# Leaving out the discarded matrix products in TensorE's waits at four layer-norm joints

## What is computed

```python
def layer_norm(x, g, b):
    mu = jnp.mean(xf, axis=-1, keepdims=True)
    var = jnp.mean(jnp.square(xf - mu), axis=-1, keepdims=True)
    return ((xf - mu) * lax.rsqrt(var + LN_EPS)).astype(x.dtype) * g + b

def post_norm_update(x, y, gate, res_w, g, b):
    return layer_norm(DN_ALPHA * x + res_w * gate * y, g, b)
...
    for i in range(DEPTH):                      # DEPTH = 2
        x = half_step_ffn(x, m[:, 0], m[:, 1], m[:, 2], ffn_w_in[i, 0], ...)
...
        hx = modulate(x, m[:, 3], m[:, 4])      # then neighbourhood attention (i = 0) or a short convolution (i = 1)
        x = post_norm_update(x, y_lat, m[:, 5], 1.0, ln_g[i, 1], ln_b[i, 1])
...
        x = half_step_ffn(x, m[:, 6], m[:, 7], m[:, 8], ffn_w_in[i, 1], ...)
    return x
```

## Time and profile before

| | |
|---|---|
| median of 3 runs | 2214.93 us (2208.83 to 2223.72) |
| profiled execution | 2212.52 us, of which the span from the first to the last instruction is 2210.7 us |
| TensorE busy | 2142.8 us (97%) |
| GpSimd busy | 1686.9 us (76%) |
| ScalarE busy | 1069.2 us (48%) |
| VectorE busy | 967.0 us (44%) |
| mean granted TensorE clock | 0.994 of full speed |

### The profile page before, as it was taken

The page is one execution under the profiler, slowest core; times in us unless marked ns, Lnnn a source line. Parts: engine busy times, 40 slices in busy tenths (PEclk is TensorE's granted clock), DMA queues, the critical chain, the costliest instruction groups (busy, mean ns, idle before and its releaser), DMA issues.

```text
span 2210.7 us, 32169 instructions
## 1 busy us (share of the span) xinstructions
PE 2142.8 (97%) x10197; PEld 1736.7 (79%) x10197; DVE 967.0 (44%) x1892; ACT 1069.2 (48%) x1646; POOL 1686.9 (76%) x1361
## 2 busy tenths in 40 slices
PE   9999999999999999999999999999999999999997
PEld 7787788777877887788778877787887788787886
DVE  7456676754556544553544442454112210434112
ACT  5555444355644543544544354555444444445442
POOL 6546498876464987888798888627988888797986
PEclk9999999999999999999999999999999999999999
DMA  7635487854344777777787865424665566464663
GB/s 257 166 106 191 153 282 244 290 176 143 108 170 153 273 260 297 255 267 264 278 284 257 314 203 165 146 75 143 195 200 186 165 186 212 140 218 146 197 205 118
DMA packets 135862, 447.10 MB, mean 202 GB/s; under 512 B 22538, under 2 KB 28130, under 8 KB 135768
## 3 DMA queue, kind: packets, MB, share of 16 engines
q1 hardware_dynamic: 130232, 427.24, 58.3%
q10 hardware_dynamic: 5536, 18.61, 2.4%
HBM read 444.60 MB, written 3.03 MB: 202 GB/s over the span
## 4 chain that ended last, share of the span: by engine, by line
POOL 50%; issue 26%; PE 21%; DVE 2%; POOLq 1%; ACT 0%; DMA 0%; SPq 0%; ACTq 0%; DVEq 0%
POOL w_lo L811 49%; PE ps L2155 6%; PE ps L2157 6%; PE ps L2156 6%; PE ps L2665 1%; PE ps L2653 1%; PE ps L2630 1%; PE ps L2493 1%; POOLq L194 0%; PE ps L2626 0%; POOL ada_land L857 0%; POOLq L809 0%; PE ps L2596 0%; PE ps L2406 0%; DMA cols<-cols_dram 0%
## 5 line engine op out<-in xcount | busy, mean ns | idle before, releaser
L811 POOL TENSOR_TENSOR w_lo<-land,w_hi 128x512 fp32r<-128x512 f32 x1300 | 1650.4, 1305 | 474.4 <-ACT w_hi L916 473.3
L916 ACT ACTIVATE w_hi<-land 128x1024 fp32r<-128x1024 f32 x654 | 692.4, 1061 | 914.8 <-PE ps L2157 692.8
L2155 PE MATMUL ps<-w_hi,h_hi 128*128 128x512 f32 (+1 forms) x1840 | 730.9, 397 | 37.4 <-DVE h_lo L1500 22.0
L2157 PE MATMUL ps<-w_hi,h_lo 128*128 128x512 f32 (+1 forms) x1840 | 718.6, 391 | 0.0
L2156 PE MATMUL ps<-w_lo,h_hi 128*128 128x512 f32 (+1 forms) x1840 | 717.7, 390 | 0.0
L2155 PEld LDWEIGHTS ps<-w_hi,h_hi 128*128 128x128 f32 x1840 | 346.6, 188 | 128.1 <-issue 40.2
L2157 PEld LDWEIGHTS ps<-w_hi,h_lo 128*128 128x128 f32 x1840 | 346.6, 188 | 73.6
L2156 PEld LDWEIGHTS ps<-w_lo,h_hi 128*128 128x128 f32 x1840 | 347.2, 189 | 67.3
L1542 DVE TENSOR_TENSOR hid_lo<-ps,hid_hi 128x512 f32 (+1 forms) x77 | 53.2, 691 | 548.3 <-ACT hid_hi L1056 548.3
L2155 PE MATMUL ps<-w_hi,hid_hi 128*128 128x512 f32 x616 | 245.4, 398 | 1.5 <-POOL w_lo L811 1.5
L2156 PE MATMUL ps<-w_lo,hid_hi 128*128 128x512 f32 x616 | 243.5, 395 | 0.0
(11 more groups left out here) (276 smaller groups left out, 1910.8 us busy)
## 6 DMA issues: line engine op xcount, KB each, us to landing
land<-ffn_w_in_dram SPq DMA_DIRECT2D x220, 512.0 KB, 3.6
ada_land<-ada_w_dram SPq DMA_DIRECT2D x144, 512.0 KB, 5.2
land<-ffn_w_out_dram SPq DMA_DIRECT2D x110, 512.0 KB, 3.9
land<-w_ffn_in_dram SPq DMA_DIRECT2D x88, 512.0 KB, 4.0
land<-w_ffn_out_dram SPq DMA_DIRECT2D x44, 512.0 KB, 4.6
land<-na_w_qkv_dram SPq DMA_DIRECT2D x40, 512.0 KB, 4.0
land<-w_xkv_dram SPq DMA_DIRECT2D x32, 512.0 KB, 3.5
land<-w_in_dram SPq DMA_DIRECT2D x32, 488.0 KB, 4.2
```

The costliest lines, as they stand in the source:

```text
L811: done = pool.tensor_tensor(w_lo[:, slot, half], land[:, slot, half], w_hi[:, slot, half].bitcast(F32), ALU.subtract)
L916: act.activation(w_hi[:, slot, :], land[:, slot, :], ACT.Copy).then_inc(*my.up("hi_ready"))
L2155: pe.matmul(dst, lh, wh, start=first, stop=False)
L2157: done = pe.matmul(dst, ll, wh, start=False, stop=last)
```

## The change

All three counts become zero, so `hold` issues nothing. No other instruction, wait or transfer is touched.

```diff
-HELD = (2, 2, 1)
+HELD = (0, 0, 0)
```

## The result

| | before | changed |
|---|---|---|
| median | 2214.93 us (2208.83 to 2223.72) | 2227.47 us (2224.36 to 2233.47) |
| profiled execution | 2212.52 us, span 2210.7 us | 2227.47 us, span 2225.7 us |
| TensorE busy | 2142.8 us | 2142.2 us |
| mean granted TensorE clock | 0.994 | 0.983 |

Five runs of each kernel give a changed kernel that is 0.52% slower, ratio 1.0052 with a 95% interval of 1.003 to 1.0074; the two medians are 12.5 us apart. The 19.1 us of held products are gone from TensorE, and its busy time is nearly what it was, because other products got longer.

A forecast was written before the change was run, and what follows sets the result against it. TensorE, busy 97% of the span, was taken to bound the kernel. Falls of 6.4 and 1.9 us, less 0.5 us given back, on 2212.52 us gave 2220.3 us, put at 2221 us; range 2210 to 2233 us.

The forecast's parts named there:

- the held products cost nothing and leave no gain: At the four joints: 19.1 us of held work lies inside waits set by ACT and DVE; removal gains 0.
- one stretch costs 1.6 us over dense products: Behind idle waits: a 3.4 us stretch at half clock slows 8 products by 0.20 us each, 1.6 us.
- I count one fall at each of the four joints: First and second wait around the transposes: one low-clock stretch per joint, 1.6 us each, 6.4 us in all.
- my second rival: Low clock for two stretches at each joint, all third waits falling too: 20.8 us, 2233 us; chance 0.10.
- slowed transposes: Transposes of tile 0 at low clock would delay DVE by 0.4 us, counted only in the 3.6 us upper bound.
- the third waits, 1.2 falls and 1.9 us: Waits of 1.84 us before tile 1: 0.3 falls a joint, 1.2 falls at 1.6 us each, 1.9 us.
- what is given back: Waits for POOL's `w_lo` about 15 us behind the joints absorb some delay: 0.5 us, bounds 0 and 1.5 us.
- the case that I gave 0.70: One low stretch at most joints, some behind the third waits: 2216 to 2226 us; chance 0.70.
- The added low time: Sign in the changed profile: added low-clock time over TensorE's work, divided by two, should equal the added span.
- one sign of being wrong: The prediction would be wrong if the clock fell at places far from the joints.
- Slower by over 1%: Rival: over 22 us lost, needing one low stretch beyond 44 us or all four beyond 11; chance 0.02.
- a low clock of 50 us: Skill's warning of a gate stuck slow: 25 us lost from one fall, 2238 us; not expected in this trace.

The follow-up runs named there:

- the still background: Kernel with all other waits held but the four joints empty, against the kernel before: ratio 1.0019, median 2220.32 us; 10.9 us above the same kernel with joints held.
- the version with (2, 2, 1): Also the held version: kernel before plus held products in RMS joint and attention waits, three moved to the 3.3 us wait: ratio 0.9962, median 2209.43 us.
- the version with (1, 1, 1): One held product at each place of the four joints, all other waits held, against the kernel before: ratio 0.9961, median 2210.25 us.

## Why the prediction was right or wrong

**Right: the held products cost nothing and leave no gain.** No wait became shorter without them, and the one joint without a fall in the kernel with the third wait empty lost 0.0 us.

**Right: the loss is the clock's, and one stretch costs 1.6 us over dense products.** Three joints with the third wait empty showed 1.6 us at the 16th to 20th product, and three with the second wait empty lost 1.57, 1.64 and 1.61 us.

**Wrong in size: "I count one fall at each of the four joints", 6.4 us.** A fall did come at each joint, but it was priced as one stretch, and the pair cost 9.9 us alone. Two stretches in a row came at all four joints, in the profile of the change as in that of the kernel with only the pair empty, and at three of four against the still background; the change had a third in a row at its fourth joint. The mechanism of my second rival, which I had given 0.10, is what happened; only its price of 3.6 us a joint was too high as a rule (the change lost 3.3 us at its fourth joint, with three stretches), since part of the first stretch lay in the wait, at the fourth joint of that kernel 3.1 of 3.4 us: the pair cost 2.05 to 2.90 us a joint when alone. I had read the five stretches of the trace as the form that a fall has. But those waits had dense work behind them, and here a second idle wait followed the first. With either of the two filled, the doubles were gone in seven of eight cases. Yet the second empty wait can't be the whole cause. The kernel with only the second wait empty had a double at its third joint, and the kernel with one product at each place had two elsewhere, behind single waits of 1.80 and 3.37 us with dense work behind them. What all 14 stretches of 6.8 us or more outside the neighbourhood attention have in common is that 0.6 to 2.5 us of waiting lies inside them, as 1.0 us does at the first joint of the change; the low stretches that lie wholly over products are all single there. Why the clock then stays low for longer is open.

**Named, but not put into the sum: slowed transposes.** I had 0.4 us for them in the upper bound alone. Where the clock was low under the transposes of tile 0, at the second and the fourth joint of the change, its first product came 0.20 and 0.43 us later after them than before; at the other two joints there was no such delay.

**Nearly right, by two errors that cancel: the third waits, 1.2 falls and 1.9 us.** There were two falls behind third waits with all left out, three with only the third empty and two against the still background, so 7 of 12, and not the 0.3 a joint that I took from the RMS joints. But the net loss was only 1.5 us for three.

**Wrong: what is given back.** I took 0.5 us for all four joints, from brackets of 0.47 us. A late TensorE got back 1.3 us behind the second and the third joint and 0.7 us behind the first. The two waits whose brackets say 0.25 and 0.47 us are 1.24 us from start to start. And it is given back only behind a fall at the third wait: in the change at the second and the fourth joint, where only the pair's stretches delayed TensorE, both waits for GpSimd are still there, here the second of them at the second joint, which answers to the earlier trace rows:

```profile
1739.72 0.50 PE L2155 MATMUL ps<-w_hi,h_hi 128*128 128x512 f32 x1 [0.46 <-POOL w_lo L811]
```

Slots of the ring are freed by the products of tile 1, so a delay in tile 0 delays ACT and GpSimd as well. That it is this which makes the difference was argued from the code and not tried.

**The sum.** Predicted 7.8 us over the profiled execution of before, measured 11.8 us from the first joint on, 12.5 us between the medians, and 10.9 us against the still background. The median of 2227.47 us is inside the range of 2210 to 2233 us and 6.5 us above the forecast. But it is inside only because the range reached up to the double stretches; it lies above the 2216 to 2226 us of the case that I gave 0.70, and two of the five runs, at 2233.47 us, reach just past the range.

**The signs that I had named.** The low clock behind every second wait, the 0.43 us and two falls behind third waits came as forecast. The added low time was to be twice the added span: at the joints it is 31.0 us over TensorE's work, half of it 15.5 us. Of that 2.0 us was given back behind the first and the third joint, and low time over the transposes costs only in part, which leaves the 11.8 us in reach. The waits for GpSimd are gone behind the third joint, and still there behind the second and the fourth. And one sign of being wrong came true by its words: the clock fell at places far from the joints, at 889 us and for longer in the attention. Kernels with the joints held show the same there, so it doesn't belong to the change; I should have asked for more low time than such kernels have.

**Slower by over 1%, and a low clock of 50 us.** The median is well below that; the two slowest runs are 0.8% above the median of before. The longest low stretch while TensorE worked was 20.5 us, in the attention of the kernel with the RMS joints held, about half of the 44 us at which I had set that rival, and six times what the rows of one trace had shown me. The 50 us that the Trainium skill warns of ("TensorE: Matmul & The Clock Gate", section "Part 1: The HAM clock gate") came up in no profile here. The Trainium skill's words there are that the gate was "stuck at K=1/4", which I took for the half-speed state; read as a quarter of full speed, my estimate from that page would have been 37.5 us and not 25. Every low stretch in these profiles is at 0.50.

## What to carry to other kernels

Where an engine with a gated clock waits between dense stretches, what counts is what stands behind the wait and whether a second wait follows: one stretch of 3.4 us at half clock costs 1.6 us over dense products and 0.5 to 0.6 us where most of it lies over discarded work, and two waits of over 2 us with eight transposes between them brought two in a row at 11 of 12 joints. One discarded product of 0.85 us in each wait of the joints was enough here (8 of 8 joints in two profiles), at no cost that could be seen, as long as it ends before the wait does; look in the timeline that it really stands where the queue waits. And price a stall from start to start, not by its bracket, before deciding how much of a delay it will take back.

## What the runs showed of the hardware that was not expected

**Short vector instructions beside GpSimd.** Spans of otherwise like kernels differ by 5 us from the first 40 us on, and the cause is in the start. Six of the 14 profiles have the longer one. These are DVE's rows of the version with (2, 2, 1), whose profiled execution took 2205.25 us:

```profile
19.84 0.18 DVE L1439 TENSOR_SCALAR ang<-ang 128x32 f32<-128x32 f32 x1
20.05 0.18 DVE L1440 TENSOR_SCALAR ang<-ang 128x32 f32<-128x32 f32 x1
20.27 2.66 DVE L1442 SCALAR_TENSOR_TENSOR ang<-ang 128x32 f32<-128x32 f32 x3
```

and of the version with (1, 1, 1), at 2210.25 us:

```profile
21.24 1.21 DVE L1439 TENSOR_SCALAR ang<-ang 128x32 f32<-128x32 f32 x1
22.48 1.21 DVE L1440 TENSOR_SCALAR ang<-ang 128x32 f32<-128x32 f32 x1
23.73 3.74 DVE L1442 SCALAR_TENSOR_TENSOR ang<-ang 128x32 f32<-128x32 f32 x3
```

GpSimd's rows in the same two profiles:

```profile
20.31 13.96 POOL L811 TENSOR_TENSOR w_lo<-land,w_hi 128x512 fp32r<-128x512 f32 x11 [19.33 <-ACT w_hi L916]
```

```profile
19.87 12.63 POOL L811 TENSOR_TENSOR w_lo<-land,w_hi 128x512 fp32r<-128x512 f32 x10 [18.89 <-ACT w_hi L916]
```

An instruction of 0.18 us takes 1.21 us once GpSimd's instructions of 1.3 us are running. In the first profile GpSimd starts late enough that the first five of this chain (two of L1438, L1439, L1440 and the first of L1442) are through at full speed; in the second it starts 0.44 us earlier and DVE 0.4 us later, and only the first is. Four more instructions lengthened by 1.03 us each and the 0.4 us make up most of the 4.6 us by which DVE's `zin` comes later. Not every short instruction is hit: in the first profile a chain of twelve on 128x2 (L1391 to L1399, all of them reading or writing PSUM) kept 0.15 to 0.17 us each from 28.28 us on, with GpSimd busy all the while. What decides it wasn't tried. TensorE then waits for DVE for 3.28 us at 36.69 us, and its clock falls there:

```profile
36.69 3.24 PE L2513 MATMUL ps<-ident,io 128*128 128x128 f32 x16 [3.28 <-DVE zin L1568]
```

The first joint comes at 1500.00 us in the one and at 1505.06 us in the other. That the two groups in the runs of the held version, five at 2204.9 to 2206.6 us and seven at 2209.2 to 2211.0 us, are these two cases fits their distance, but only profiled executions show it.

**Longer low stretches in thin work.** Behind the same wait of 1.5 us in the neighbourhood attention, the profiles show stretches of 3.4, 10.2, 13.7 and 20.5 us, and none in the kernel with the first wait empty. Behind single waits with dense products behind them they were 3.4 us long, with three exceptions of 6.8 us. That it is the short products of the attention that keep the clock low once it has fallen is argued from this and not tried.
